# A delta rule's triangular inverse whose transposed factor VectorE makes by 32x32 transposing

## The reference, cut to what matters

```python
def rwkv7_scan(r, w, k, v, kk, a):
    def step(state, inp):
        sa = jnp.einsum('bhvk,bhk->bhv', state, -kk_t)
        state = (state * w_t[:, :, None, :]
                 + sa[..., None] * (kk_t * a_t)[:, :, None, :]
                 + v_t[..., None] * k_t[:, :, None, :])
        return state, jnp.einsum('bhvk,bhk->bhv', state, r_t)
```

## Time and profile before

| what | value |
|---|---|
| median of 3 runs | 3341.71 us (3339.03 to 3342.1) |
| the profiled execution's own time | 3340.39 us |
| its span | 3338.4 us |
| TensorE busy | 3271.3 us (98%) |
| VectorE busy | 1747.3 us (52%) |
| ScalarE busy | 1189.8 us (36%) |
| GpSimd busy | 411.3 us (12%) |
| granted TensorE clock, mean | 0.989 |

### The profile page before, as it was taken

The page is one execution under the profiler, slowest core; times in us unless marked ns, Lnnn a source line. Parts: engine busy times, 40 slices in busy tenths (PEclk is TensorE's granted clock), DMA queues, the critical chain, the costliest instruction groups (busy, mean ns, idle before and its releaser), DMA issues.

```text
span 3338.4 us, 44425 instructions
## 1 busy us (share of the span) xinstructions
PE 3271.3 (98%) x18534; PEld 2613.3 (78%) x18534; DVE 1747.3 (52%) x2533; ACT 1189.8 (36%) x1884; POOL 411.3 (12%) x318
## 2 busy tenths in 40 slices
PE   8999999999999999999999999999999999999999
PEld 6777678887777888887777788888888887678887
DVE  7854456844447443347767644434464335554333
ACT  4344434534443422233333342222353224342221
POOL 0000012001001311112322111100011001011110
PEclk9999999999999999999999999999999999999999
DMA  6732123322122233232100023332323222023332
GB/s 236 227 104 67 54 95 114 114 87 66 57 84 68 89 95 100 96 118 94 58 2 2 27 70 118 95 98 91 101 82 101 95 89 88 11 73 95 100 96 82
DMA packets 83911, 295.47 MB, mean 89 GB/s; under 512 B 9472, under 2 KB 12800, under 8 KB 81664
## 3 DMA queue, kind: packets, MB, share of 16 engines
q1 hardware_dynamic: 78384, 270.61, 25.4%
q10 hardware_dynamic: 5328, 22.02, 2.1%
HBM read 283.94 MB, written 8.65 MB: 88 GB/s over the span
## 4 chain that ended last, share of the span: by engine, by line
PE 88%; DVE 6%; ACT 2%; issue 2%; POOL 1%; DMA 0%; DVEq 0%; ACTq 0%; POOLq 0%
PE acc L479 70%; PE acc L1521 1%; PE aux L1506 1%; DVE w_lo L390 1%; PE acc L3274 1%; PE acc L2500 1%; PE aux L3238 1%; PE aux L1802 1%; PE acc L1833 1%; PE acc L2504 1%; PE acc L2490 1%; PE aux L1820 1%; PE aux L2457 1%; PE acc L2004 1%; PE aux L1993 1%
## 5 line engine op out<-in xcount | busy, mean ns | idle before, releaser
L479 PE MATMUL acc<-op_hi,w_hi 128*128 128x512 f32 x2624 | 1077.0, 410 | 12.6 <-ACT ssd_soft L1287 3.8
L383 ACT ACTIVATE w_hi<-raw 128x1024 fp32r<-128x1024 f32 (+2 forms) x476 | 494.3, 1038 | 1539.0 <-PE acc L479 1528.7
L479 PE MATMUL acc<-op_hi,w_lo 128*128 128x512 f32 x2624 | 1026.4, 391 | 0.0
L479 PE MATMUL acc<-op_lo,w_hi 128*128 128x512 f32 x2624 | 1024.9, 391 | 0.0
L390 DVE TENSOR_TENSOR w_lo<-raw,w_hi 128x1024 fp32r<-128x1024 f32 (+2 forms) x476 | 575.8, 1210 | 303.6 <-ACT w_hi L383 303.3
L479 PEld LDWEIGHTS acc<-op_hi,w_hi 128*128 128x128 f32 x2624 | 494.5, 188 | 140.1 <-issue 39.7
L479 PEld LDWEIGHTS acc<-op_hi,w_lo 128*128 128x128 f32 x2624 | 493.8, 188 | 106.4
L479 PEld LDWEIGHTS acc<-op_lo,w_hi 128*128 128x128 f32 x2624 | 495.1, 189 | 104.2 <-issue 10.1
L479 PE MATMUL acc<-ffn_hi,w_hi 128*128 128x512 f32 x800 | 311.4, 389 | 0.0
L479 PE MATMUL acc<-ffn_hi,w_lo 128*128 128x512 f32 x800 | 311.2, 389 | 0.0
L479 PE MATMUL acc<-ffn_lo,w_hi 128*128 128x512 f32 x800 | 311.2, 389 | 0.0
(11 more groups left out here) (589 smaller groups left out, 3891.5 us busy)
## 6 DMA issues: line engine op xcount, KB each, us to landing
raw<-in_w SPq DMA_DIRECT2D x436, 512.0 KB, 3.5
late_ada<-in_ada ACTq DMA_DIRECT2D x32, 512.0 KB, 4.2
raw<-in_w SPq DMA_DIRECT2D x32, 384.0 KB, 3.0
ada<-in_ada ACTq DMA_DIRECT2D x4, 1024.0 KB, 14.4
ada<-in_ada SPq DMA_DIRECT2D x4, 1024.0 KB, 21.8
x_mid<-x SPq DMA_DIRECT2D x16, 256.0 KB, 2.9
x<-x_mid SPq DMA_DIRECT2D x2, 2048.0 KB, 7.7
skew<-rel_rows SPq DMA_DIRECT2D x12, 192.0 KB, 3.2
```

Source lines behind the costliest of these rows:

```text
L383: act.activation(self.w_hi[g % AHEAD][:, 0:k, :], self.raw[s][:, 0:k, :], ACT.Copy).then_inc(self.split_hi.handle, 1)
L479: mm = pe.matmul(self.bank(s, g), w[:, k, :], a[:, k, 0:s.n], start=(k == 0 and q == 0), stop=(k == k_tiles - 1 and q == 2))
```

## The change

The second group of each level's "second" (L2504) and the update of D (L2797) go, and so does the masked product that starts X. X now lies in packed blocks like D during the levels (`packed_x`), so that its update is one instruction. VectorE makes D from X after each level by its transposing of 32x32 blocks (`dve.transpose`), at level 5 of the one off-diagonal block that is still needed. At the start D is a copy of the identity (GpSimd) into which the level-0 part of A is copied under a mask, and X is its transpose; both are done by VectorE between the copies of product 0. ScalarE unpacks X into its chunks after level 5. D has its own buffers, which alternate between pairs. Four products take the planned times of five: for pairs 2 to 5 product i is at tB - 4.96 + 1.61 i, the turns stay where they were against tB. The table of constants loses 128 columns (`level0_t`). The core of the diff:

```diff
...
-    AT = {"front": -37.16, "products": 33.65, "product": 1.61, "turns": 1.0, "turn": 3.1, "bonus": 23.11,
+    AT = {"front": -37.16, "products": 32.2, "product": 1.61, "turns": 4.06, "turn": 3.1, "bonus": 23.11,
...
-          "product_kept": 0.18, "turn_kept": 1.08, "start": -6.96, "diagonal": 0.75, "edge_level": 5.35,
+          "product_kept": 0.18, "turn_kept": 1.08, "base": -0.6, "edge_level": 5.35,
...
-          "early_head": 2.8, "early_second": 2.14, "early_update": 1.17, "early_copy": 0.95, "gap": 3.34,
+          "early_head": 2.8, "early_second": 2.14, "early_update": 1.17, "early_copy": 0.95, "gap": 4.8,
...
+        self.packed_x = [core.place(f"inv_x{i}", [P, T], 80 + 2 * i)[:, :] for i in range(2)]
+        later_d = core.place("inv_d", [P, T], 84)[:, :]
...
+        self.D = [[blocks(ap, e) for e in range(2)] for ap in (core.ss[0][:, :], o[1][:, 0, :], later_d)]
...
-        return ((self.A[m % 2], kkq, bh, "strict"), (self.X[m % 2], bh, kkq, "level0_t"), (ak, kh, kkq, "strict_t"),
+        return ((self.A[m % 2], kkq, bh, "strict"), (ak, kh, kkq, "strict_t"),
                 (rb, bh, rq, "incl"), (rk, kh, rq, "incl"))
 
     def product_banks(self, m, i):
 
-        return self.swap_banks if m and i % 2 == 0 and (m > 1 or i) else self.front_banks[::-1]
+        if m == 1:
+            return (self.front_banks[::-1], self.core.acc[0:2], self.front_banks[::-1], self.swap_banks)[i]
+        return self.swap_banks if m and i % 2 == 0 else self.front_banks[::-1]
...
                 elif m == 1 and i == 1:
-                    pe.wait_ge(*self.kept.ge(10 * m + 2))
+                    pe.wait_ge(*self.linear.last_freed(self.segment))
                 elif m == 1 and i == 2:
+                    pe.wait_ge(*self.kept.ge(8 * m + 2))
+                elif m == 1 and i == 3:
                     pe.wait_ge(*self.updated.ge(self.level_count(0, self.LEVELS, 1)))
                 elif i >= 2:
-                    pe.wait_ge(*self.kept.ge(10 * m + 2 * (i - 1)))
+                    pe.wait_ge(*self.kept.ge(8 * m + 2 * (i - 1)))
...
                     if level == 1:
-                        pe.wait_ge(*self.kept.ge(10 * m + 3 + e))
+                        pe.wait_ge(*self.x_set.ge(2 * m + e + 1))
...
-                            mm = pe.matmul(block(first_banks[e], n, i), block(C[e], n, i), diagonal(X[e], n, i),
+                            mm = pe.matmul(block(first_banks[e], n, i), block(C[e], n, i), block(X[e], n, i),
...
                     if level == 1:
-                        pe.wait_ge(*self.d_set.ge(4 * m + 2 * e + 2))
-                    bank = next_banks[e]
+                        pe.wait_ge(*self.d_set.ge(2 * m + e + 1))
+                    else:
+                        pe.wait_ge(*self.flipped.ge(self.pick_count(m, level - 1, e)))
                     for n in range(NT):
                         for i in range(2):
-                            mm = pe.matmul(self.packed(bank, level, 0, rows[i], n), block(D[e], n, i),
+                            mm = pe.matmul(self.packed(next_banks[e], level, rows[i], n), block(D[e], n, i),
                                            self.columns_of(block(G[e], n, i), level, 1), start=True, stop=True)
-                    for n in range(NT):
-                        for i in range(2):
-                            mm = pe.matmul(self.packed(bank, level, 1, rows[i], n), block(G[e], n, i),
-                                           self.columns_of(block(D[e], n, i), level, 0), start=True, stop=True)
                     mm.then_inc(*self.second.inc())
...
+        def unpacks(m):
+            X, full = self.x_blocks(m), self.X[m % 2]
+            for e in range(2):
+                yield self.level_time(m, self.LEVELS, e) + self.pace_of(m, "second") + 0.5
...
+                act.wait_ge(*self.updated.ge(self.level_count(m, self.LEVELS - 1, e)))
+                for i, rows in enumerate((slice(0, HD), slice(HD, P))):
+                    ins = act.activation(self.diagonals_of(full[e], i), self.blocks(X[e])[rows, :, :], ACT.Copy)
+                ins.then_inc(*self.unpacked.inc())
...
                     dve.tensor_copy(self.blocks(self.below[m % 2][e])[HD:P, :, :], chunks(bank[:, :])[HD:P, :, 0:HD]
                                     ).then_inc(*self.kept.inc())
+                    dve.wait_ge(*self.kept.ge(8 * m + e + 1))
+                    dve.wait_ge(*self.based.ge(2 * m + e + 1))
+                    D = self.inverse_parts(m)[0][e]
+                    dve.copy_predicated(self.blocks(D), tiled(core.c("level0").bitcast(U32), NT), self.blocks(dst)
+                                        ).then_inc(*self.d_set.inc())
+                    dve.wait_ge(*self.d_set.ge(2 * m + e + 1))
+                    dve.transpose(self.x_blocks(m)[e], D).then_inc(*self.x_set.inc())
...
                     dve.wait_ge(*self.second.ge(self.level_count(m, level, e)))
-                    bank, b = next_banks[e], 1 << level
-                    for i, rows in enumerate((slice(0, HD), slice(HD, P))):
-                        x = self.diagonals_of(X[e], i).rearrange("p n (k c) -> p n k c", c=2 * b)[:, :, :, b:2 * b]
-                        grown = self.packed(bank, level, 0, rows).rearrange("p (n k) b -> p n k b", n=NT)
-                        dve.tensor_tensor(x, x, grown, ALU.add)
-                    d = self.columns_of(D[e], level, 0)
-                    dve.tensor_tensor(d, d, self.packed(bank, level, 1), ALU.add).then_inc(*self.updated.inc())
+                    x = self.columns_of(X[e], level, 1)
+                    dve.tensor_tensor(x, x, self.packed(next_banks[e], level), ALU.add).then_inc(*self.updated.inc())
+                    dve.wait_ge(*self.updated.ge(self.level_count(m, level, e)))
+                    if level < self.LEVELS - 1:
+                        dve.transpose(D[e], X[e]).then_inc(*self.flipped.inc())
+                    else:
+                        dve.transpose(blocks(D[e])[b:HD, :, 0:b], blocks(X[e])[0:b, :, b:HD]
+                                      ).then_inc(*self.flipped.inc())
...
-            pool.memset(core.squares[:, 2:4, :], 0.0).then_inc(*self.zeroed.inc())
+            pool.memset(core.squares[:, 0:4, :], 0.0).then_inc(*self.zeroed.inc())
...
+            pool.wait_ge(*self.kk_done.ge(RW))
+            pool.memset(core.squares[:, 4:6, :], 0.0).then_inc(*self.zeroed.inc())
...
             for e in range(2):
-                pool.tensor_copy(chunks(self.X[m % 2][e]), ident).then_inc(*self.x_set.inc())
+                pool.tensor_copy(self.blocks(self.inverse_parts(m)[0][e]), ident).then_inc(*self.based.inc())
...
```

More of the change, by code:

```diff
@@ L2306, in inverse_parts, with x_blocks @@
     def inverse_parts(self, m):
-        return (*self.work[m > 0], *self.banks[m > 0])
+        return (self.D[m and 2 - m % 2], *self.work[m > 0], *self.banks[m > 0])
+    def x_blocks(self, m):
+        ap = self.packed_x[m % 2]
+        return [ap[:, e * (T // 2):(e + 1) * (T // 2)] for e in range(2)]
     def bonus_time(self, m):
@@ L2356, in packed @@
     @staticmethod
-    def packed(bank, level, which, rows=slice(0, P), n=None):
-        b, w, at = 1 << level, HD // 2, which * (T // 4)
-        ap = bank[rows, at:at + NT * w] if n is None else bank[rows, at + n * w:at + (n + 1) * w]
+    def packed(bank, level, rows=slice(0, P), n=None):
+        b, w = 1 << level, HD // 2
+        ap = bank[rows, 0:NT * w] if n is None else bank[rows, n * w:(n + 1) * w]
         return ap.rearrange("p (k b) -> p k b", b=b)
@@ L2510, in inverse @@
                 for n in range(NT):
[L2511 removed]
+                    mm = pe.matmul(block(first_banks[e], n, 0), block(below[e], n, 1), block(X[e], n, 1),
                                    start=True, stop=True)
@@ L2689, in last_norm @@
                            ).then_inc(*self.rooted.inc())
-        return (kk(), *(f(m) for m in range(RW) for f in (front, turns, inverse, sequence, last_norm)))
+        return (kk(), *(f(m) for m in range(RW) for f in (front, turns, inverse, unpacks, sequence, last_norm)))
     def dve(self, dve):
@@ L2800, in inverse @@
                 dve.wait_ge(*self.second.ge(self.level_count(m, self.LEVELS, e)))
-                dve.tensor_copy(chunks(X[e])[0:HD, :, HD:P], self.blocks(next_banks[e][0:HD, :])
+                if m == 1 and e == 0:
+                    dve.wait_ge(*self.zeroed.ge(7))
+                dve.tensor_copy(chunks(full[e])[0:HD, :, HD:P], self.blocks(next_banks[e][0:HD, :])
                                 ).then_inc(*self.updated.inc())
@@ L2891, in picks @@
                                        ).then_inc(*self.picked.inc())
-        def diagonals(m):
-            A, D, blocks = self.A[m % 2], self.inverse_parts(m)[0], self.blocks
-            for e in range(2):
-                yield self.tB[m] + self.AT["diagonal"] + 1.2 * e
-                pool.wait_ge(*self.kept.ge(10 * m + 1 + e))
-                if m > 1:
```

(8 more changed lines are left out.)

67 lines of the change are left out of this document (35 added, 32 removed).

## The result

The changed kernel takes 3370.62 us (median of 4 runs, 3364.3 to 3375.4), the kernel before 3341.29 beside it (4 runs): ratio 1.0089, 95% interval 1.0074 to 1.0104. It is **slower by 0.9%**, some 29 us, where 0.56% faster was forecast. The profiled execution took 3364.3 us, the fastest of the four.

What follows compares the result with a forecast made beforehand. In the delta-rule stage, TensorE's list was taken as most of the chain, VectorE's as the rest. Terms summed to -18.6 us from the profiled 3340.39, giving 3321.8, or 3323 us for the median; range 3312 to 3345.

Steps and rivals of the forecast that it cites:

- pair 1's boundary: 1666.39 to 1686.97 us, at half clock: product 2 waits instead of product 1, a product and an L2504 go; -2.7 us.
- one rival with a chance of 0.13: Clock falls in each boundary's new wait until the first turn: +8 us a boundary, +32 over four, 3355 us; chance 0.13.
- zeroing ahead of the stage: GpSimd's zeroing before the delta-rule stage grows from 1024 to 2048 columns, in the chain; +0.9 us.
- pair 0, up to pair 1's product 0: Seven L2504 and a product go, first masked copies take longer, fewer updates follow the reciprocal; -6.0 us.
- boundary of pairs 2 and 4: Product 0 to first turn: 2.7 us new wait ahead of product 2, less 1.56 removed; +1.14 us each.
- boundary of pair 3: Product 0 to first turn, same sum as for pairs 2 and 4, at full clock; +1.14 us.
- boundary of pair 5: Product 0 to first turn, the same new wait but two L2504 removed there; +0.7 us.
- rest of the period: First turn to next pair's product 0: five L2504 groups and four cheaper updates; -2.85 us, four times, -11.4.
- the last pair's levels and end: Eight L2504 leave the chain from 1864 to 1887.83 us, level-6 part held by others; -3.5 us.
- The rival of a slow transposing: VectorE's transposing at 0.73 us gives +7.5, 3331; at 1.25 us +21, 3344; chance of 0.9 us or more: 0.1.
- the fourth rival: TensorE's list gets shorter but another wait takes the gain up at each step; 3340 us, chance 0.08.
- Everything costed at nothing: GpSimd's identity copies and missing level-0 work, ScalarE's unpacking, 64 KB less of constants (under 0.2 us): taken as 0.

Runs made afterwards that it cites:

- combo_fill: combo_pair0 plus one idle 128x512 matmul on TensorE in the pause ahead of chunk 1's correction, pairs 0 to 3; 3323.49 us, ratio 0.9937 to the kernel before.
- combo: Changed kernel with first solve again between products 1 and 2, product 0 copied out before D and X work, part of the zeroing later; 3339.49 us, ratio 0.9991.
- combo_pair0: combo with pair 0's turns and levels planned 1.79 us later, where they stood before the change; ratio 0.9968 to the kernel before.
- fill_levels: Changed kernel plus 16 idle matmuls on constants at every level where L2504's group stood; 3374.06 us, ratio 1.0091 to the kernel before.

## Why the prediction was wrong

The step that failed is the one behind the terms: **all but pair 1's boundary were summed at the full clock**, and a fall of the clock was put into one rival with a chance of 0.13, for the boundary alone. The runs showed 82 us more at half clock instead, worth 31 to 35 of the 42 us between forecast and result. Point by point, by shifts of the same instruction between the two traces:

| step | forecast, us | measured, us |
|---|---|---|
| zeroing ahead of the stage | +0.9 | +0.85 (1514.47 to 1515.04, with the stage's start 0.28 earlier) |
| pair 0, up to pair 1's product 0 | -6.0 | +6.3 (1666.39 to 1673.27, less the 0.57 before it) |
| pair 1's boundary | -2.7 | -3.0 |
| boundary of pairs 2 and 4, clock held | +1.14 | +1.24 (13.54 against 12.30) |
| boundary of pair 3, clock fell | +1.14 | +5.85 (18.15 against 12.30) |
| boundary of pair 5, clock fell | +0.7 | +7.2 (21.13 against 13.96) |
| rest of the period, pairs 2 and 4 (13.7 us at half clock in it) | -2.85 | +1.9 (33.61 against 31.69) |
| rest of the period, pairs 1 and 3 | -2.85 | -1.7, -1.4 |
| the last pair's levels and end | -3.5 | +3.5 (shift of +20.1 at its first turn, +23.6 at the next projection) |

*Prices, right.* The transposing (0.445 for 0.44), the update, the boundary's wait (2.7 for 2.7), its list on VectorE, the net of +1.14 where the clock held. The rival of a slow transposing is out.

*The clock at the boundary, half right.* It fell at two boundaries of four in this execution, and it cost 4.6 us in pair 3 (18.15 - 13.54), where the rival had 8, since it came back before the first turn; in pair 5 the boundary was 6.5 us over the forecast. (The rival's own readings are a little off: 9.6 us at 1.87 times are 18.0, not 17.6, and the shares in the earlier trace rows put its half-clock stretch at 1660.3 to 1680.8, not 1660.67 to 1680.4. Neither moves a chance.) The Trainium skill (TensorE: Matmul & The Clock Gate, HAM oscillation — how this bites in real kernels) describes a kernel whose clock falls again and again in waits for the next operand; it is the pattern of this trace, though what is waited for here is VectorE and not a transfer, and the waits are of 1.64 and 2.74 us where the page draws some 3 to 5.

*The clock in mid-period, not foreseen at all.* The sum counted L2504 only as a cost. It was also what kept TensorE busy between a level's first matmuls and the correction behind a front's scan: with it the longest such wait was 1.2 us, without it 1.8. (That a shorter list only makes another wait longer was the fourth rival's mechanism; its 3340 us left out what the longer wait does to the clock.) combo_fill shows the term as it would have been: its last two steady periods are 41.36 and 41.38 us (product 0 at 1748.34, 1789.70 and 1831.08) against 43.99 before, a saving of 2.6, of which 29.2 against 31.69 lies outside the boundary: -2.5 where the sum had -2.85.

*Pair 0, the wrong sign.* The sum took -2.5 for levels that start 1.8 us earlier, "only two" updates behind the reciprocal. Two updates do stand behind it, but the reciprocal itself comes at 1663.04 instead of 1654.14, and the level-6 part stands still for 4.2 us until the first of them is done. Later levels give that back (combo to combo_pair0, -0.23%). The rest of the 12 us by which this step was off came earlier, while the projection ran: the shift against the kernel before is 0.6 us at 1515.04, 2.3 at pair 0's product 0 (1578.34 to 1580.68; 6.8 us at half clock lie before it), 4.0 at the next product (its wait of 3.6 for 1.3), 4.6 at the first turn and 7.0 at the projection's last matmul (1652.65 to 1659.62), with new stretches of 3.4 us at half clock at 1588.6 and 1643.2.

*Everything costed at nothing* (GpSimd's copies, ScalarE's unpacking, the constants) showed no wait of its own in TensorE's list.

Where the 42 us between forecast and result (-18.6 and +23.7) went: 82 us more at half clock in the stage, at the measured 0.38 to 0.43 us each, are 31 to 35. (Half of the 82 would be 41 and close the sum by itself; that would be the price if TensorE's list were the chain in all of these stretches, and over whole executions the measured one is lower.) The other 7 to 11 us weren't taken apart; pair 0's longer waits (3.6 for 1.3, and 4.2 at level 6) are the nearest candidates. In combo_fill the clock is that of the kernel before (76 us against 77 over all runs) and the time is 21 us less, near the forecast's 18.6. That is partly luck, since combo_fill's boundary, zeroing and pair 0 are ordered otherwise than in the kernel that was forecast.

## What to carry to other kernels

An instruction on the busiest engine can pay for itself: before taking small matmuls out, look at the pause that they leave, and at what the stretch behind it would cost at half clock; ask it of every term of the sum, not of one. A small wait in a stage of small matmuls is to be priced with the stretch behind it: here 2.7 us of waiting cost 4.6 more, and 5.2 us less of waiting, 0.4 to 1.0 in each of six places, was worth some 24. And where an order can't be had without a pause, one idle matmul in it (1.1 us in a pause of 1.64) was worth 10 us, while the same matmul a few groups later gave nothing.

## What was not expected of the hardware

The clock fell behind pauses of 1.64 us in a stretch with small matmuls on both sides, while it held over the 3 us window with TensorE idle for most of it in the kernel before, which had dense matmuls ahead of it; with 3.7 us in the same place in the changed kernel it fell (half clock from 1513.5 to 1520.3). Of equal pauses some let it fall and some don't: in the changed kernel the boundaries of pairs 2 and 4 held and those of 3 and 5 didn't, while the pauses in the middle of these periods were followed by 13.7 us at half clock where the boundary had held and by 3.4 us where it hadn't (pair 3). With the middle kept busy (fill_levels) all four boundaries fell. Why they alternate is open. Two executions of one program differed by 17 us in their time at half clock, and by 7 us in length.
